# Regrouping the token tiles of two requests between two passes over the weights of a hybrid encoder layer

## What is computed

```python
def encoder_layer(x, ...):                         # once for each request
    proj = rms_norm(x, g_mix) @ w_in               # 2048 x 10240: q, k, v of both mixers, then two gates
    ... # heads normalised and rotated; 16 attention units of 128 or 256 queries
    merged = sigmoid(ga) * (oa @ w_br_a) + sigmoid(gb) * (ob @ w_br_b)
    x = x + merged @ w_out
    return x + peer(rms_norm(x, g_ffn), ...)

def peer(h, w_pq, sub_keys, u_emb, v_emb):         # h: 256 x 2048
    q = (h @ w_pq).reshape(t, 8, 2, 128)
    s = einsum('thcd,hcnd->thcn', q, sub_keys)     # 8 heads, two lists of 128 scores
    v1, i1 = top_k(s[:, :, 0], 16); v2, i2 = top_k(s[:, :, 1], 16)
    cv, ci = top_k(v1[..., :, None] + v2[..., None, :], 16)    # of 256 sums
    e = i1[ci // 16] * 128 + i2[ci % 16]           # 128 experts of 16384 for each token
    a = einsum('ckd,cd->ck', u_emb[e], h)
    return einsum('ck,ckd->cd', gelu(a) * softmax(cv), v_emb[e])
```

## Time and profile before

| what | value |
|---|---|
| device time, median of 3 runs | 4192.55 us (4192.25 to 4193.02) |
| span of the profiled execution | 4193.2 us |
| busy: TensorE, VectorE, ScalarE, POOL | 3546.2, 3103.5, 1421.7, 835.7 us |
| moved by DMA | 1099.78 MB, mean 262 GB/s |
| in it: gathered rows (queue q0), SP's and ScalarE's loads and stores (q1, q10) | 536.90, 561.35 MB |

### The profile page before, as it was taken

One profiled execution on the slowest core, in us unless ns is written; L12 is line 12 of the kernel. 1 busy time (PEld: TensorE's weight loads), 2 busy tenths in 40 slices (PEclk: granted clock), 3 DMA queues, 4 the chain that ended last, 5 costly groups with the idle time before them and its releaser, 6 DMA issues.

```text
span 4193.2 us, 60957 instructions
## 1 busy us (share of the span) xinstructions
PE 3546.2 (85%) x22046; PEld 3217.2 (77%) x22046; DVE 3103.5 (74%) x3905; ACT 1421.7 (34%) x1936; POOL 835.7 (20%) x772
## 2 busy tenths in 40 slices
PE   7997988852996338978888867999998999999998
PEld 6876987752775228976888857997887999998886
DVE  4654444468898777877789999887787777777786
ACT  4544433321443113333432201334442233333443
POOL 0000000000223543222111266222221012121221
PEclk9999998986998668989999956999998699999999
DMA  5651655532998888989877856998886188888887
GB/s 188 193 162 51 181 152 174 176 110 107 355 333 318 302 317 329 362 321 329 314 266 289 297 179 210 337 360 311 330 329 245 55 320 313 302 313 307 327 332 293
DMA packets 288251, 1099.78 MB, mean 262 GB/s; under 512 B 24832, under 2 KB 25216, under 8 KB 219008
## 3 DMA queue, kind: packets, MB, share of 16 engines
q1 hardware_dynamic: 208640, 528.55, 37.1%
q0 software_dynamic: 73728, 536.90, 33.8%
q10 hardware_dynamic: 5760, 32.80, 2.1%
HBM read 1087.67 MB, written 10.49 MB: 262 GB/s over the span
## 4 chain that ended last, share of the span: by engine, by line
PE 63%; DVE 14%; issue 11%; DMA 4%; POOL 4%; ACT 2%; DVEq 0%; ACTq 0%; PEldq 0%; POOLq 0%; PEld 0%; SPq 0%
PE ps L1083 17%; PE ps L1135 13%; PE ps L1307 13%; PE ps L1079 9%; PE ps L1280 5%; PE ps L1118 4%; POOL rows L305 3%; DVE rows L638 3%; DMA w<-v_emb 2%; DVE w_lo L655 2%; DVE pick L981 1%; DMA w<-w_out 1%; DVE w_lo L622 1%; ACT w_hi L327 1%; DMA gvec<-g_ffn_b 1%
## 5 line engine op out<-in xcount | busy, mean ns | idle before, releaser
L622 DVE TENSOR_TENSOR w_lo<-w,w_hi 128x1024 fp32r<-128x1024 f32 x752 | 918.9, 1224 | 642.4 <-ACT w_hi L327 589.9
L327 ACT ACTIVATE w_hi<-w 128x1024 fp32r<-128x1024 f32 x752 | 795.9, 1060 | 1244.6 <-PE ps L1083 375.3
L303 POOL TENSOR_TENSOR tick<-iota 128x1 f32<-128x1 f32 x256 | 167.8, 655 | 3201.0 <-DVE acc L642 1246.0
L638 DVE CUSTOM_DVE_ANT_0 rows<-rows,h 128x2048 f32<-128x2048 f32 x256 | 583.6, 2284 | 33.2 <-DMA rows<-u_emb,stage_i 31.2
L642 DVE SCALAR_TENSOR_TENSOR acc<-rows,stage_d,acc 128x2048 f32<-128x2048 f32 x256 | 600.3, 2345 | 6.5 <-DVE stage_d L633 5.4
L655 DVE TENSOR_TENSOR w_lo<-ps,w_hi 128x1024 fp32r<-128x1024 f32 x256 | 312.2, 1220 | 170.4 <-ACT w_hi L394 167.6
L394 ACT ACTIVATE w_hi<-ps 128x1024 fp32r<-128x1024 f32 x256 | 262.9, 1028 | 434.5 <-PE ps L1118 421.7
L305 POOL DMA_INDIRECT rows<-v_emb,stage_i x256 | 348.9, 1363 | 57.4 <-issue 39.3
L305 POOL DMA_INDIRECT rows<-u_emb,stage_i x256 | 318.8, 1246 | 57.7 <-issue 41.0
L1135 PE MATMUL ps<-ht_hi,w_lo 128*128 128x256 f32 x2048 | 292.3, 286 | 37.8 <-DVE w_lo L655 37.5
L1079 PE MATMUL ps<-w_lo,ht_hi 128*128 128x512 f32 x1024 | 281.3, 397 | 40.7 <-DVE w_lo L622 40.7
(11 more groups left out here) (180 smaller groups left out, 5157.5 us busy)
## 6 DMA issues: line engine op xcount, KB each, us to landing
w<-w_in SPq DMA_DIRECT2D x320, 512.0 KB
w<-u_emb SPq DMA_DIRECT2D x256, 512.0 KB
w<-v_emb SPq DMA_DIRECT2D x256, 512.0 KB
w<-w_out SPq DMA_DIRECT2D x64, 512.0 KB
w<-w_pq SPq DMA_DIRECT2D x64, 512.0 KB
w<-w_br_b SPq DMA_DIRECT2D x32, 512.0 KB
xin<-x ACTq DMA_DIRECT2D x4, 2048.0 KB, 8.9
w<-w_br_a SPq DMA_DIRECT2D x16, 512.0 KB
```

What stands on the lines that cost most here:

```text
L327: act.activation(w_hi[:, j % 2, :, :], w[:, j % RING, :, :], ACT.Copy).then_inc(hi_ready, 1)
L622: dve.tensor_tensor(w_lo[:, j % 2, :, :], w[:, j % RING, :, :], w_hi[:, j % 2, :, :].bitcast(F32), ALU.subtract).then_inc(lo_ready, 1)
L638: dve.tensor_tensor_reduce(out=row, in0=row, in1=h2[0][:, t, :], scale=1.0, scalar=0.0, op0=ALU.mult, op1=ALU.add, accum_out=stage_d[:, j: ...
```

## The change

The tokens are grouped anew from the gates to the queries. The first pass takes the first request through the projection and attention, and then its tile 0 alone through gates, branches, output, normalisation and queries. The second pass takes the second request through projection and attention, and then tiles 2, 3 and 1 together through the rest. Both passes stream the same 248 slabs. All streams are in rows form: a slab has 6 matmuls of 512 columns for each tile. Banks 0 to 5 hold two sets of up to three accumulators, banks 6 and 7 all turned groups, which are put between slabs; so q and k are turned during the projection.

Tile 0's selection runs on VectorE beside the first 44 slabs of the second projection; the selections of tiles 1, 2, 3 run at the end beside the early table blocks. The turns are taken tile by tile, both tables of tile 0 and then of tile 1, by a quota for each slab; in the second attention 10 are left, beside the selections at the end and beside the picks none. POOL issues one gather for each turn straight from the index table, without the `tick` instruction. There are no barriers before the picks, and every loop is written out.

The diff, cut to its core:

```diff
+PASS_TILES = ((0,), (2, 3, 1))
+ATT_TURNS = (0, 1, 1, 1, 0, 1, 1, 0, 1, 1, 0, 1, 1, 0, 1, 0)
+TOPK0_SLABS = 44
...
+def plan_segments():
...
+        for ct in range(QKV_CT):
+            add(st["qkv"], "qkv", ct, 8, NT)
+        for ct in range(4):
+            for kind, slabs in (("ga", 8), ("ba", 2), ("gb", 8), ("bb", 4)):
+                add(st["mix"], kind, ct, slabs, nt)
+        for name in ("out", "pq"):
+            for ct in range(4):
+                add(st[name], name, ct, 8, nt)
...
+def plan_turns():
...
+    q1 = STAGES[1]["qkv"][0].g0
+    run(q1 + TOPK0_SLABS, q1 + 96, 0.33)
+    state["taken"] += sum(ATT_TURNS)
+    mix, out, pq = (STAGES[1][n][0].g0 for n in ("mix", "out", "pq"))
+    run(mix, out, 1.02)
+    run(out, pq + 32, 1.08)
+    for h in range(HALVES):
+        run(U_G0[h] + (2 * EARLY if h == 0 else 0), V_G0[h], 0.97)
+        run(V_G0[h], V_G0[h] + 2 * HB, 0.56)
...
         def _(sp):
...
+                if p == 1:
+                    load_ahead = STAGES[1]["mix"][0]
+                    for j in range(RING):
+                        load(views["in"][j, :, :, first_col["ga"]:first_col["ga"] + CT], load_ahead.g0 + j)
+                    sp.wait_ge(sc_ready, N_UNITS + 8)
+                    sp.dma_start(x_src[3][:, :, :], x[0].rearrange("(t p) d -> p t d", p=P)[:, 1:2, :]).then_inc(x_in[3], 16)
...
         def _(pool):
...
-                pool.wait_ge(used, K * 8 + (8 * GROUPS * table + j + 2))
-
-                pool.tensor_tensor(tick[:, j // 2:j // 2 + 1], iota[:, 0:1], iota[:, 0:1], ALU.add).then_inc(ticked, 1)
...
+            for n in range(TURNS):
+                tile, table, k = n // (2 * SEL), n // SEL % 2, n % SEL
+                if n % (2 * SEL) == 0:
+                    pool.wait_ge(staged, tile + 1)
+                need(pool, used, n - ROWS + 1)
+                pool.indirect_dma_start(rows[:, n % ROWS, :], None, (u_emb, v_emb)[table],
+                                        bass.IndirectOffsetOnAxis(ap=eidx[:, tile, k:k + 1], axis=0)).then_inc(row_in[n % ROWS], 16)
...
         def _(act):
...
+                    if p == 1 and seg.ct == 10:
+                        act.wait_ge(topk_done, 1)
...
+            attention(0)
+            act.dma_start(x_src[1][:, :, :], xs[1]).then_inc(x_in[1], 16)
+            act.dma_start(g_vec[1][:, :], g_mix_b).then_inc(g_in[1], 16)
+            act.dma_start(x_src[2][:, :, :], xs[0][:, 0:1, :]).then_inc(x_in[2], 16)
+            act.dma_start(g_vec[2][:, :], g_ffn_b).then_inc(g_in[2], 16)
...
+            for k, t in enumerate((1, 2, 3)):
+                n0, n1 = EARLY * k // 3, EARLY * (k + 1) // 3
+                u_blocks(0, n0, n1 - n0, 0)
+                act.wait_ge(shifted, 2 + k)
+                act.activation(gsel[:, t, :], gsel[:, t, :], ACT.Exp).then_inc(exped, 1)
...
         def _(dve):
...
+            def qkv1_slab():
+                i = at_slab[0]
+                g = STAGES[1]["qkv"][0].g0 + i
+                lo(g)
+                qkv_step(1, i)
+                turns(QUOTA.get(g, 0))
+                at_slab[0] += 1
...
+            topk(0, 0, 0, beside_qkv1)
+            while at_slab[0] < TOPK0_SLABS:
+                qkv1_slab()
+            topk_weights(0, 0, 1)
...
+            def beside_u(us):
+                spent[0] += us
+                while early[0] < min(spent[0] / 162.0, 1.0) * 2 * EARLY:
+                    lo_turned(U_G0[0] + early[0])
+                    early[0] += 1
+            for k, t in enumerate((1, 2, 3)):
+                topk(1, t, t % 2, beside_u)
...
+                for i in range(2 * (HB - b0)):
+                    g = U_G0[h] + 2 * b0 + i
+                    lo_turned(g)
+                    if i % 2 and i > 1:
+                        weigh(b0 + i // 2 - 1)
+                    turns(QUOTA.get(g, 0))
...
         def _(pe):
...
+            def slab(seg, j, lhs, k0):
...
                     for kk in range(SK):
...
+                        for t in range(seg.tiles):
+                            ins = pe.matmul(ps[:, seg.bank + t, :], lhs(t)[:, half, k, :], wt[:, g % 2, kk, :],
...
+            qkv(0)
+            attention(0)
+            mix(0)
+            out(0)
+            pq(0)
+            pe.wait_ge(turn_lo, GR["n1"][-1].count)
+            qkv(1)
+            attention(1)
...
+            mix(1)
+            out(1)
+            pq(1)
```

More of the change, by code:

```diff
@@ L2 @@
+from collections import namedtuple
 import numpy as np
@@ L25 @@
 SK = 2
-SPC = KC // SK
 RING = 4
@@ L55, with qk_slab, add @@
 N_OUT = 12
+PASS_TILES = ((0,), (2, 3, 1))
+OT_SLOTS = (slice(0, 2), slice(0, 3, 2))
+OT_OF = ((0,), (0, 2, 1))
+Segment = namedtuple("Segment", "kind ct g0 n tiles bank side count")
+Group = namedtuple("Group", "kind banks index count before")
+def qk_slab(u):
+    return 90 if u == N_QK - 1 else 16 * (u // 2) + 33 + 2 * (u % 2)
 def out_of(u):
     return u // 2 if u < 8 else u - 4
+def plan_segments():
+    stages, g, n = [], 0, 0
+    count = {"act": 0, "dve": 0}
+    def add(stage, kind, ct, slabs, tiles):
+        nonlocal g, n
+        side = "dve" if kind in ("ba", "bb", "out") else "act"
+        count[side] += 1
+        stage.append(Segment(kind, ct, g, slabs, tiles, 3 * (n % 2), side, count[side]))
+        g += slabs
+        n += 1
+    for p in range(2):
+        st = {name: [] for name in ("qkv", "mix", "out", "pq")}
+        nt = len(PASS_TILES[p])
+        for ct in range(QKV_CT):
[6 more added lines that the diff above has]
+                add(st[name], name, ct, 8, nt)
+        stages.append(st)
+    return stages, g
@@ new lines, with take, run @@
+STAGES, W_SLABS = plan_segments()
+GR = plan_groups()
+U_G0 = [W_SLABS + 4 * HB * h for h in range(HALVES)]
+V_G0 = [W_SLABS + 4 * HB * h + 2 * HB for h in range(HALVES)]
+ATT_TURNS = (0, 1, 1, 1, 0, 1, 1, 0, 1, 1, 0, 1, 1, 0, 1, 0)
+TOPK0_SLABS = 44
+def plan_turns():
+    quota, ends = {}, {}
+    state = dict(taken=0, credit=0.0, hold=-1)
+    def take(g, m):
+        for _ in range(m):
+            if state["taken"] == TURNS or (g is not None and g < state["hold"]):
+                break
+            quota[g] = quota.get(g, 0) + 1
+            state["taken"] += 1
+            state["credit"] -= 1
+            if state["taken"] % SEL == 0:
+                ends[state["taken"] // SEL - 1] = g
+                if state["taken"] // SEL % 2:
+                    state["hold"] = g + 5
+                    break
+    def run(g0, g1, rate):
+        for g in range(g0, g1):
+            state["credit"] += rate
+            take(g, min(int(state["credit"]), 2))
+    q1 = STAGES[1]["qkv"][0].g0
[7 more added lines that the diff above has]
+        run(V_G0[h], V_G0[h] + 2 * HB, 0.56)
+    rest = TURNS - state["taken"]
+    return quota, ends, rest
@@ L669, in _ @@
[L669 to L686 removed]
+            dve.memset(eps_c[:, :], EPS).then_inc(eps_ready, 1)
@@ L1059, in _, with free @@
             pe.wait_ge(consts_in, 96)
[L1060 to L1068 removed]
+            def free(gr):
+                for kind, n in gr.before:
+                    pe.wait_ge(sides(kind), n)
```

1809 lines of the change are left out of this document (970 added, 839 removed).

## The result

The changed kernel takes 3877.4 us, the median of four runs (3875.4 to 3885.6), against 4192.4: a ratio of 0.9258, interval 0.9244 to 0.9271, 315 us less. The forecast was 3816, 61 us too low and inside its own range of 3750 to 3880 as well as the wide one. The profiled execution spans 3876.7 us.

What follows compares the result with a forecast made beforehand. TensorE bounded the weight and table streams, while VectorE's selection and turns stretched the other stages. Fifteen stage times, with DMA limiting stages with turns, summed to 3816 us; own range 3750 to 3880, wide range 3650 to 3975.

Steps and rivals of the forecast that it cites:

- one-tile pass: First pass, gates to queries, one tile: 152 slabs at 1.65 us, plus 12 normalisation and 10 inputs, 273 against 504.
- second projection: Second request's projection with one tile's selection and 17 turns beside it: 303 us, bounds 276 and 344.
- first and second attention: First attention stays at 66 us; second, with 10 turns and the third tile's turned groups, 94 against 228.
- its output and queries: Three-tile pass after gates and branches: 285 us, with 34 more around the pass elsewhere in the sum split as 24 and 15.
- final selection: Three tiles' selection at the end beside 64 table slabs, no turns: 3 x 92 = 276 us, bounds 240 and 300.
- late U0, U1: First table's streams per expert half, the first only behind its early blocks: 263 and 526 us, limited by DMA.
- V0, V1: Second table's streams per expert half, 128 slabs each with 71 and 69 turns: 378 and 372 us, limited by DMA.
- The rate of DMA: In stages with turns DMA becomes the limit, at 375 GB/s between bounds 358 and 414.
- the first rival: Stages with turns: TensorE stays the bound, DMA feeding 383 to 411 GB/s; 137 us less, 3680; chance 0.20.
- The second rival: Stages with turns: DMA holds no more than 358 GB/s; 104 us more, 3920, or 3964 with upper prices; chance 0.20.
- The third rival: First pass: one-tile slabs cost 2.7 us like two-tile ones, or the clock drops; 160 us more, 3976; chance 0.07.
- The fourth rival: Ring of four gathered rows: late landings stop TensorE; 4495 us at a landing of 20 us; chance 0.05.

Runs made afterwards that it cites:

- the two undo runs: Changed kernel with 80 turns instead of 10 in the second attention: 4054.0 us; changed kernel with the first tile's selection not interleaved with projection slabs: 3920.8 us.
- The estimate of 124: Changed kernel with the estimate that deals table slabs out beside the last three selections set to 124 us instead of 162: 3827.2 us.

## Why the prediction came out as it did

| step | forecast | measured |
|---|---|---|
| one-tile pass | 273 | 314 |
| second projection | 303 | 298 |
| first and second attention | 66 + 94 | 76 + 109 |
| three-tile gates and branches | 372 | 364 |
| its output and queries | 285 | 305 |
| final selection | 276 | 318 |
| late U0, U1 | 263 + 526 | 241 + 493 |
| V0, V1 | 378 + 372 | 374 + 376 |

**Right:** the mechanism of the gain. Selection off TensorE's path, turns out of the attention and beside slabs that have room; the two undo runs give 177 and 43 of the 315 us back. The second projection came within 5 us. The 68 us at the first picks, the moved normalisation, the rows form, the written-out loops and the missing `tick` were not undone alone; what each is worth is not shown.

**The rate of DMA** was mis-sized, and with it the limit of the long streams named wrongly. I took 375 GB/s. To keep TensorE's pace the gates asked for 383 and got 383; the U stretches asked for 411 and got 400 and 401, over 241 and 493 us; at a full share with TensorE relieved, DMA gave 387 and 404. U slabs took 3.77 and 3.85 us, next to the 3.75 that I had named as the sign of the first rival. So in gates and U that rival, TensorE stays the bound, describes what happens, with DMA one to three per cent behind it. The second rival, 358, is out. The Trainium skill, "DMA: Bandwidth & Descriptors", Specifications, gives about 358 GB/s as HBM's limit for one core; the traces here show 404 over 487 us, and the measurement decides. I had weighed that line alone. The Trainium skill, "HBM Reference", Specifications (TRN2), calls it the share of a core whose neighbour streams too, and states about 425 GB/s for a core alone; one core runs here, and 404 at a full share lies under that figure.

**V0 and V1** came within 4 us of the forecast, but not by a rate of 375. V0 ran at 386, and with six slots it fell to 360 us at 397 GB/s, close to the 355 of TensorE's work. Most of what stretched V0 was the depth of the ring; that this and my rate came to the same time is luck.

**One-tile slabs**, taken as 1.65: 1.97. My bounds priced three engines' hand-over and a rate of DMA, and left out the latency of a ring: landing, high and low part, over four slots. Slabs land in 4.7 to 5.2 us in this pass, so (4.7 + 1.06 + 1.22)/4 to (5.2 + 1.06 + 1.22)/4, 1.75 to 1.87 us a slab. (The 5.5 that I used in the expectation, for 1.95, is more than the landing here.) The 0.1 to 0.2 above it were not separated.

```profile
w<-w_in SPq DMA_DIRECT2D x64, 512.0 KB, 4.7
w<-w_out SPq DMA_DIRECT2D x32, 512.0 KB, 5.2
```

Two more slots brought 1.72 to 1.80; a third buffer brought nothing. The third rival (2.7, or a low clock) is out: the clock was 0.96.

**The final selection:** I saw that the slabs would run out of turn, and priced it at 92 us a tile; it was 106. 5.5 us a tile of that is VectorE waiting for ScalarE's exponentials (the wait shown above), which my sum lacked; how the rest divides was not separated. The estimate of 124 shows what the whole misdealing cost: 58 us in the stretch, 50 of the whole time.

**Attention:** boundaries misread. I cut the first attention of before at 322 us; its first score matmul starts earlier, as the timeline of the kernel before shows, and the gates' first matmul at 387.93: 73.4 us, not 66.

```profile
314.49 2.86 PE L1178 MATMUL ps<-raw 128*128 128x256 f32 x12 [0.75 <-ACT raw L450]
```

The second attention of before was cut worse: I read its length from 1367 and its turns from 1390, 35 and 58 us late, and so counted 60 turns in 205 us where there are 80 in 264. (264 - 73.4)/80 is 2.4 us a turn; my (205 - 66)/60 came to 2.3 because both cuts were short, which is luck. The second projection of before is 296 us by the same correction, so its 344, my upper bound and my sign of a selection that does not fit, was no mark to measure against. Without turns the second attention of after takes 88.6, against 76 to 79 for the first, so the normalisation and turned groups of the third tile cost 9 to 13 us and not 5.

**Output and queries:** 20 us over. In the output stretch slabs land in 15.6 us while ScalarE's 5.2 MB of inputs come in:

```profile
w<-w_out SPq DMA_DIRECT2D x9, 512.0 KB, 15.6
```

TensorE is not the limit there, as 14 matmuls a slab leave the stretch at 158 us, and ScalarE waits 44 us for slabs of `w_out`, so DMA is the likely one; seven fewer turns, which shorten the stretch by 14, relieve VectorE too and do not part the two. The 15 us I had allowed covered only the end of the pass.

**The fourth rival**, the ring of rows, is out at 9 to 12 us of landing, against 17.5 for its break-even. VectorE hardly waits for rows (6.5 us in all for the second table), where I had expected it to. Three rows cost up to 26 us; five were not tried.

The errors upward (one-tile pass, selection, attentions, output and queries: 128 us) met 63 downward in U and gates, and with small ones the sum came out 61 low. It lay in its range partly because errors of both signs met.

## What to carry to other kernels

When work of a second engine is to be hidden, look for the stretch whose step is long enough to hold it: 70 turns cost 2.4 us each in a serial chain and 2 us in all beside slabs of 4.1 us. Before a stage is priced from windows, cut them where its first and last instruction stand. When a stream's step becomes shorter, price the ring by latency (landing and use, over the slots) as well as by rate and by engine: a rate that fits the time need not be what holds it, as V0 shows. A hand-written interleave that runs on estimates should use the sum of what it spends: 162 for 124 cost 50 us.

## What had not been expected of the hardware

DMA of this one core gave 404 GB/s at a full share for 487 us, with two thirds of the bytes, 128.65 of 196.80 MB, as gathered rows. A stretch with TensorE idle in pieces of up to 33 us was granted 0.90 of the clock, and 0.99 once the same work was dealt out evenly. With one row fewer in flight a gather lands sooner, in 9.0 to 9.1 instead of 10.7 to 11.2 us, so a shorter ring costs far less than the landing at full depth would say.
